# A sparse gate table built with matmuls: one-hots per token on GpSimd and the product into H with tokens innermost

## The chip, the cores and the metric

The kernel runs on one core of a Trainium2 chip. The metric is device time in microseconds (us) of that core, the median of three runs.

## The reference, cut to what matters

The program is one decoder layer of 256 tokens and 1024 channels: a token mixer (attention branches, projections), a layer norm, then a retrieval over 128 x 128 = 16384 single-neuron experts, and a second layer norm. The change lies in the retrieval:

```python
s_top, i_top = lax.top_k(s, K)                      # K = 16 of 128 keys, twice (p = 0, 1), 8 heads
cand = s_top[:, :, 0, :, None] + s_top[:, :, 1, None, :]
best, pos = lax.top_k(cand, K)                      # 16 experts (i, j) per token and head
gate = jax.nn.softmax(best, axis=-1)
hid = gelu(x . u_tab[expert])                       # one number per token and expert
out = sum over the experts of gate * hid * v_tab[expert]
```

The kernel doesn't gather. It computes `hid` for all 16384 experts (dense), builds for each token n the 128 x 128 table G[j, i], the sum of the gates of the token's 128 picks (8 heads x 16) that chose expert (i, j), multiplies `hid` by it, and multiplies the product by all of `v_tab`.

## The kernel before, in words

Five engines run their own instruction streams, ordered by semaphores only. The stages that matter here are three.

- Stage U (128 tiles of `u_tab`). SP loads a tile into `raw`, ScalarE rounds it into `whi` (`split_hi`, L471), VectorE and GpSimd subtract to get `wlo` (`split_lo`, L728 on VectorE for 768 columns, L323 on GpSimd for 256), and TensorE does three matmuls per product (L1173 to L1175). ScalarE writes gelu into `H[j, i, n]`, laid out per partition j as 128 rows i of 256 tokens n, so that neighbouring i lie 1024 bytes apart and neighbouring n 4 bytes. VectorE does the top-k between.
- The gate stage. At its start VectorE copies the transposed picks from PSUM to `selT` (i and j of every pick, one pick per partition, tokens in the free dimension, bf16) and `gateT` (L1104, L1105). Then it goes by blocks of 8 tokens (`BLK`), 32 in all. For a block, VectorE's `hots` (L1066) compares a bf16 iota, stored eight times over (`iota8`), with i and j of the picks, one instruction of 2048 elements that writes both one-hots into `raw_ij` with the token innermost. GpSimd's `scale_j` (L435) multiplies the j one-hots of six tokens by the gate and writes them as fp32 in token order into `hot_j`; ScalarE's `scale_hots` does this for the other two tokens (L673, after copying their gates, L669) and casts the i one-hots into `hot_i` (L670). TensorE's `gate_tables` (L1444) does one 128x128x128 fp32 matmul per token, `hot_j` stationary and `hot_i` moving, into two PSUM banks of a block (the trace shows two records per matmul, so 16 per block). VectorE's `into_h` (L1079) multiplies the 8 x 128 numbers of the block into `H`, walking i innermost in PSUM and in `H`.
- Stage V (128 tiles of `v_tab`): ScalarE and VectorE split `H` into `hhi` and `hlo`, TensorE does L1464 to L1466.

`hot_i` and `hot_j` have two buffers each (`HOTS`), the PSUM side four (`GB`), `raw_ij` two. The hot buffers lie on the memory of `ahi` and `alo`, the stationary side of stage U, so they are written only after the last tile of U (`tiles_used` of `T_V`). A buffer is free again when the block's matmuls are done (`g_done`). In VectorE's loop `hots(n+3)` stands before `into_h(n+1)`. Beside the first blocks run the splits of the first three tiles of V. Stage V begins when the last block's matmuls are issued, `g_used` says that block 28's product is in `H`, and `first_hi` and `first_lo` (the split of the first 128 tokens, L702 and L1119) are there.

Of the kernel before, what the change touches and what calls it, by code (L numbers as in the profile page):

```python
# [23 lines left out]
BF16 = mybir.dt.bfloat16  # L24
U32 = mybir.dt.uint32
ACT = mybir.ActivationFunctionType
AX = mybir.AxisListType

P = 128
SEQ, D = 256, 1024  # L30
# [4 lines left out]
AHEAD = NS - 1  # L35
# [7 lines left out]
PH, NK, TOPK = 8, 128, 16  # L43
# [109 lines left out]
def layer(nc, x, xT, w_lr, w_tiles_in, w_tiles_out, w_tiles_q, w_tiles_u, w_tiles_v, w_decay,  # L153
# [5 lines left out]
    def place(name, shape, dt=F32, alias=None):  # L159
# [3 lines left out]
        if alias is None:  # L163
# [64 lines left out]
    selT = place("selT", [P, 2, SEQ], BF16)  # L228
    gateT = place("gateT", [P, SEQ])
    iota8 = place("iota8", [P, P, BLK], BF16)  # L230
    gate8 = place("gate8", [P, HOTS, BLK])
    gdiff = place("gdiff", [P, NT * P])
    gsum = place("gsum", [P, NT * PH])
    hot_at = at[0]
# [14 lines left out]
    raw_ij = [place(f"raw_ij{b}", [P, 2, P, BLK], BF16, alias=hot_at + b * hot_size) for b in range(HOTS)]  # L249
    at[0] = max(at[0], hot_at + 2 * hot_size)  # L250
# [21 lines left out]
             "sc_copied hid_used r_neg r_exp half_done sel_done sel_tp selT_done iota8_ready hot_ready "  # L272
             "j_scaled hots_wide g_done g_used first_hi first_lo w_hi w_lo out_ready stored dve_own "
# [9 lines left out]
    def spare_hold(e, sem, value):  # L283
        hold(e, sem, value, S["spare"])
# [32 lines left out]
    def _(pool):  # L317
# [98 lines left out]
        pool.wait_ge(S["ln_done"], 2)  # L416
        pool.tensor_copy(iota8[:, :, :], iota[:, :, None].to_broadcast([P, P, BLK])).then_inc(S["iota8_ready"], 1)
# [6 lines left out]
        def scale_j(n, b, i=None):  # L424

            if i is None:
                pool.wait_ge(S["hot_ready"], n + 1)
                if n >= HOTS:
                    pool.wait_ge(S["g_done"], n + 1 - HOTS)
                g = gateT[:, n * BLK:n * BLK + POOL_TOKS]  # L430
            else:
                pool.wait_ge(S["hot_ready"], i * GB + (b + 1))
                spare_hold(pool, S["g_done"], i * GB + (b + 1 - HOTS))
                g = gateT[:, bass.ds(i * (GB * BLK) + b * BLK, POOL_TOKS)]
            pool.tensor_tensor(hot_j[b % HOTS][:, 0:POOL_TOKS, :],  # L435
                               raw_ij[b % HOTS][:, 1, :, 0:POOL_TOKS].rearrange("p j n -> p n j"),
                               g[:, :, None].to_broadcast([P, POOL_TOKS, P]), ALU.mult)\
                .then_inc(S["j_scaled"], 1)
# [3 lines left out]
        for n in range(GB):  # L442
            scale_j(n, n)
            if n == 1:
                split_lo(Tile(T_V + AHEAD - 1))
        with pool.Fori(1, SEQ // BLK // GB) as i:
            for b in range(GB):
                scale_j(None, b, i)
# [16 lines left out]
    def _(act):  # L465
# [192 lines left out]
        def scale_hots(n, b, i=None):  # L658

            if i is None:  # L660
                act.wait_ge(S["hot_ready"], n + 1)
                if n >= HOTS:
                    act.wait_ge(S["g_done"], n + 1 - HOTS)
                g = gateT[:, n * BLK + POOL_TOKS:(n + 1) * BLK]
            else:
                act.wait_ge(S["hot_ready"], i * GB + (b + 1))
                spare_hold(act, S["g_done"], i * GB + (b + 1 - HOTS))
                g = gateT[:, bass.ds(i * (GB * BLK) + (b * BLK + POOL_TOKS), BLK - POOL_TOKS)]
            act.activation(gate8[:, b % HOTS, 0:BLK - POOL_TOKS], g, ACT.Copy).then_inc(S["act_own"], 1)  # L669
            act.activation(hot_i[b % HOTS][:, :, :], raw_ij[b % HOTS][:, 0, :, :].rearrange("p i n -> p n i"), ACT.Copy)  # L670
            act.wait_ge(S["act_own"], own.n + n + 1 if i is None else i * GB + (own.n + b + 1))
            for k in range(POOL_TOKS, BLK):
                last = act.activation(hot_j[b % HOTS][:, k, :], raw_ij[b % HOTS][:, 1, :, k], ACT.Copy,  # L673
                                      scale=gate8[:, b % HOTS, k - POOL_TOKS:k - POOL_TOKS + 1])
            last.then_inc(S["hots_wide"], 1)

        act.wait_ge(S["selT_done"], 1)
        act.wait_ge(S["tiles_used"], T_V)
        for n in range(GB):
            scale_hots(n, n)  # L680
            if n == 1:
                split_hi(Tile(T_V + AHEAD - 1))
        with act.Fori(1, SEQ // BLK // GB) as i:
            for b in range(GB):
                scale_hots(None, b, i)
# [29 lines left out]
        own.n += SEQ // BLK  # L715
# [6 lines left out]
    def _(dve):  # L722
# [333 lines left out]
        def hots(n, b, i=None):  # L1056

            if i is not None:

                spare_hold(dve, S["hots_wide"], i * GB + (b + 1 - HOTS))  # L1060
                spare_hold(dve, S["j_scaled"], i * GB + (b + 1 - HOTS))
            elif n >= HOTS:
                dve.wait_ge(S["hots_wide"], n + 1 - HOTS)
                dve.wait_ge(S["j_scaled"], n + 1 - HOTS)
            toks = slice(n * BLK, (n + 1) * BLK) if i is None else bass.ds(i * (GB * BLK) + b * BLK, BLK)
            dve.tensor_tensor(raw_ij[b % HOTS][:, :, :, :], iota8[:, None, :, :].to_broadcast([P, 2, P, BLK]),  # L1066
                              selT[:, :, toks][:, :, None, :].to_broadcast([P, 2, P, BLK]), ALU.is_equal)\
                .then_inc(S["hot_ready"], 1)

        def into_h(n, b, i=None):  # L1070

            if i is None:
                dve.wait_ge(S["g_done"], n + 1)
            else:
                spare_hold(dve, S["g_done"], i * GB + (b + 1))
            toks = slice(n * BLK, (n + 1) * BLK) if i is None else bass.ds(i * (GB * BLK) + b * BLK, BLK)
            hv = H[:, :, toks].rearrange("p i n -> p n i")
            g = ps[:, 2 * (b % GB):2 * (b % GB) + 2, :].rearrange("p b (n i) -> p (b n) i", i=NK)
            dve.tensor_tensor(hv, hv, g, ALU.mult).then_inc(S["g_used"], 1)  # L1079
# [27 lines left out]
        dve.wait_ge(S["iota8_ready"], 1)  # L1107
        hots(0, 0)
        hots(1, 1)
        split_lo(Tile(T_V))  # L1110
        hots(2, 2)
# [11 lines left out]
        into_h(0, 0)  # L1123
        with dve.Fori(0, SEQ // BLK // GB - 1) as i:
            for b in range(GB):
                hots(b + LAG, b + LAG, i)
                into_h(b + 1, b + 1, i)
        hots(SEQ // BLK - 1, GB - 1)
        into_h(SEQ // BLK - 3, 1)
        into_h(SEQ // BLK - 2, 2)  # L1130
        dve.wait_ge(S["j_scaled"], SEQ // BLK)
        dve.wait_ge(S["hots_wide"], SEQ // BLK)
        first_lo(0)
        into_h(SEQ // BLK - 1, 3)
# [30 lines left out]
    def _(pe):  # L1165
# [268 lines left out]
        def gate_tables(n, b, i=None):  # L1434

            if i is None:
                pe.wait_ge(S["hots_wide"], n + 1)
                pe.wait_ge(S["j_scaled"], n + 1)
            else:
                pe.wait_ge(S["hots_wide"], i * GB + (b + 1))  # L1440
                pe.wait_ge(S["j_scaled"], i * GB + (b + 1))
                pe.wait_ge(S["g_used"], i * GB + (b + 1 - GB))
# [112 lines left out]
```

## Time and profile before

| | |
|---|---|
| Time, median of 3 runs | 1191.5 us (1191.3 to 1192.95) |
| Span of the profiled execution | 1190.3 us |
| Own time of the profiled execution | not listed apart from its span |
| TensorE busy | 1099.9 us (92%) |
| VectorE busy | 824.0 us (69%) |
| ScalarE busy | 623.0 us (52%) |
| GpSimd busy | 549.6 us (46%) |
| Mean granted TensorE clock | 0.989 |
| Gate stage, last matmul of U to first of V | 700.1 to 817.5 us |

The span runs from the first instruction to the last and is 1.2 us below the median of the runs, which also hold what lies around it. Engines are PE (TensorE), DVE (VectorE), ACT (ScalarE), POOL (GpSimd) and SP. A row of a group gives line, engine, operation, output and inputs, shapes, count, then busy us and mean ns of one, then the idle time in front of the instructions and who ended it. A row of a timeline gives the start and the length of an instruction or of a merged run of them (x2, x16).

### The profile page before, as it was taken

How to read it: one execution, taken by the hardware profiler on the slowest of the kernel's cores; microseconds unless marked ns; L12 is line 12 of the kernel's file. 1: busy time of each engine (PE TensorE's matmuls, PEld its weight loads, DVE VectorE, ACT ScalarE, POOL GpSimd, SP SyncE). 2: the span in 40 equal slices, each digit the busy share in tenths (PEclk: the TensorE clock that was granted, in tenths of full speed). 3: DMA queues.
4: the chain of work that ended last, by engine and by line, in shares of the span. 5: the costliest groups of instructions: out<-in, count | busy, mean ns of one | idle time of the engine just before them, and what ended most of it. 6: DMA issues, size and time to landing. Idle time of an engine off the chain costs nothing.

```text
span 1190.3 us, 21974 instructions
## 1 busy us (share of the span) xinstructions
PE 1099.9 (92%) x6734; PEld 971.3 (82%) x6734; DVE 824.0 (69%) x1329; ACT 623.0 (52%) x882; POOL 549.6 (46%) x419
## 2 busy tenths in 40 slices
PE   6999999978999999999999975557999999999995
PEld 5888887658999999999999965556888888888884
DVE  4348654564467777787777899997666666666666
ACT  4357544543455555545555578886445454454452
POOL 5474345453434333333333345554555555555554
PEclk9999999998999999999999999999999999999998
DMA  6654443343455555555555520003555555555552
GB/s 208 228 195 142 142 162 122 124 142 106 159 173 180 179 190 178 179 189 178 181 185 179 181 102 1 0 0 106 178 193 182 188 193 179 192 190 181 193 185 97
DMA packets 52456, 186.34 MB, mean 157 GB/s; under 512 B 6208, under 2 KB 6592, under 8 KB 52432
## 3 DMA queue, kind: packets, MB, share of 16 engines
q1 hardware_dynamic: 51584, 182.87, 46.1%
q0 software_dynamic: 848, 3.15, 0.7%
q8 instruction: 15, 0.25, 0.1%
q14 instruction: 9, 0.07, 0.0%
HBM read 184.94 MB, written 1.05 MB: 156 GB/s over the span
## 4 chain that ended last, share of the span: by engine, by line
PE 80%; DVE 7%; issue 6%; ACT 3%; DMA 2%; POOL 2%; DVEq 0%; ACTq 0%; SPq 0%; POOLq 0%
PE ps L1173 15%; PE ps L1175 15%; PE ps L1174 15%; PE ps L1464 10%; PE ps L1466 10%; PE ps L1465 10%; PE ps L1444 2%; DVE raw_ij L1066 2%; DMA raw<-w_tiles_in 1%; ACT hot_j L673 1%; PE ps L1213 1%; POOL wlo L323 1%; ACT whi L471 1%; DVE H L1079 1%; DVE wlo L728 1%
## 5 line engine op out<-in xcount | busy, mean ns | idle before, releaser
L323 POOL TENSOR_TENSOR wlo<-raw,whi 128x256 fp32r<-128x256 f32 x341 | 445.2, 1306 | 567.2 <-ACT whi L471 566.1
L471 ACT ACTIVATE whi<-raw 128x1024 fp32r<-128x1024 f32 x344 | 365.0, 1061 | 474.3 <-DMA raw<-w_tiles_v 178.3
L728 DVE TENSOR_TENSOR wlo<-raw,whi 128x768 fp32r<-128x768 f32 x341 | 339.1, 995 | 281.0 <-ACT whi L471 264.2
L1173 PE MATMUL ps<-ahi,whi 128*128 128x256 f32 x1152 | 328.3, 285 | 2.7 <-DVE alo L975 1.4
L1175 PE MATMUL ps<-ahi,wlo 128*128 128x256 f32 x1152 | 326.7, 284 | 0.0
L1174 PE MATMUL ps<-alo,whi 128*128 128x256 f32 x1152 | 326.7, 284 | 0.0
L1173 PEld LDWEIGHTS ps<-ahi,whi 128*128 128x128 f32 x1152 | 221.9, 193 | 3.3 <-DVE alo L975 1.8
L1174 PEld LDWEIGHTS ps<-alo,whi 128*128 128x128 f32 x1152 | 221.9, 193 | 0.0
L1175 PEld LDWEIGHTS ps<-ahi,wlo 128*128 128x128 f32 x1152 | 221.8, 192 | 0.0
L1464 PE MATMUL ps<-whi,hhi 128*128 128x512 f32 x512 | 202.5, 395 | 2.5 <-POOL wlo L323 2.5
L1465 PE MATMUL ps<-wlo,hhi 128*128 128x512 f32 x512 | 202.2, 395 | 0.0
L1466 PE MATMUL ps<-whi,hlo 128*128 128x512 f32 x512 | 202.2, 395 | 0.0
L1173 PE MATMUL ps<-whi,ahi 128*128 128x512 f32 x288 | 117.1, 407 | 11.4 <-POOL wlo L323 10.2
L1146 DVE TENSOR_TENSOR hlo<-H,hhi 128x256 fp32r<-128x256 f32 x125 | 118.2, 946 | 0.5 <-ACT hhi L696 0.5
L1464 PEld LDWEIGHTS ps<-whi,hhi 128*128 128x128 f32 x512 | 96.0, 187 | 26.5 <-DVE wlo L728 2.2
L1466 PEld LDWEIGHTS ps<-whi,hlo 128*128 128x128 f32 x512 | 96.0, 187 | 23.6
L1465 PEld LDWEIGHTS ps<-wlo,hhi 128*128 128x128 f32 x512 | 96.0, 187 | 23.4
L1444 PE MATMUL ps<-hot_i,hot_j 128*128 128x128 f32 x512 | 66.8, 285 | 50.8 <-ACT hot_j L673 49.1
L1175 PE MATMUL ps<-whi,alo 128*128 128x512 f32 x288 | 113.4, 394 | 0.0
L1174 PE MATMUL ps<-wlo,ahi 128*128 128x512 f32 x288 | 113.2, 393 | 0.0
L1444 PEld LDWEIGHTS ps<-hot_i,hot_j 128*128 128x128 f32 x512 | 61.1, 196 | 56.5 <-issue 25.6
L435 POOL TENSOR_TENSOR hot_j<-raw_ij,gateT 128x768 f32<-128x768 bf16 x32 | 62.9, 1968 | 49.2 <-DVE raw_ij L1066 47.6
(193 smaller groups left out, 1032.8 us busy)
## 6 DMA issues: line engine op xcount, KB each, us to landing
raw<-w_tiles_u SPq DMA_DIRECT2D x128, 512.0 KB, 3.3
raw<-w_tiles_v SPq DMA_DIRECT2D x128, 512.0 KB, 3.3
raw<-w_tiles_in SPq DMA_DIRECT2D x64, 512.0 KB, 3.3
raw<-w_tiles_q SPq DMA_DIRECT2D x16, 512.0 KB, 3.3
raw<-w_tiles_out SPq DMA_DIRECT2D x8, 512.0 KB, 3.3
xraw<-xT SPq DMA_DIRECT2D x4, 256.0 KB, 6.2
xt<-x POOLq DMA_DIRECT2D x1, 1024.0 KB, 5.7
out<-xt SPq DMA_DIRECT2D x4, 256.0 KB, 2.1
```

Source lines behind the costliest of these rows:

```text
L323: pool.tensor_tensor(wlo[:, tile.slot, DVE_COLS:], raw[:, tile.slot, DVE_COLS:], whi[:, tile.slot, DVE_COLS:].bitcast(F32), ALU.subtract)\
L435: pool.tensor_tensor(hot_j[b % HOTS][:, 0:POOL_TOKS, :], raw_ij[b % HOTS][:, 1, :, 0:POOL_TOKS].rearrange("p j n -> p n j"), g[:, :, None] ...
L471: act.activation(whi[:, tile.slot, :], raw[:, tile.slot, :], ACT.Copy)\
L728: dve.tensor_tensor(wlo[:, tile.slot, 0:DVE_COLS], raw[:, tile.slot, 0:DVE_COLS], whi[:, tile.slot, 0:DVE_COLS].bitcast(F32), ALU.subtract)\
L1146: dve.tensor_tensor(hlo[:, tile.slot, :], src, hhi[:, tile.slot, :].bitcast(F32), ALU.subtract)\
L1173: pe.matmul(out, ah, bh, start=start, stop=False)
L1174: pe.matmul(out, ah, bl, start=False, stop=False)
L1175: return pe.matmul(out, al, bh, start=False, stop=stop)
L1444: last = pe.matmul(ps[:, 2 * b + k // 4, (k % 4) * P:(k % 4 + 1) * P], hot_j[b % HOTS][:, k, :], hot_i[b % HOTS][:, k, :], start=True, sto ...
L1464: pe.matmul(o, hh, wh, start=start, stop=False)
L1465: pe.matmul(o, hh, wl, start=False, stop=False)
L1466: last = pe.matmul(o, hl, wh, start=False, stop=stop)
```

## The change

The one-hots get another form and other makers. GpSimd makes each token's `hot_i` in one instruction of 128 elements: compare the fp32 iota with the token's i, a per-partition scalar, and multiply by its gate, another per-partition scalar. That is eight instructions per block, 256 in all. VectorE makes `hot_j` of a block with one fp32 compare of 1024 elements, straight into the matmul's buffer and no longer with the gate. ScalarE has no part in the stage. `selT` is fp32; `iota8`, `gate8` and `raw_ij` go. VectorE's first compares now wait for the last tile of U too, and the splits of V's first tiles stand behind them. `into_h` walks the tokens innermost: in `H` runs of 8 neighbouring fp32 (32 bytes), in PSUM steps of 128 fp32 (512 bytes). It stands ahead of `hots(n+2)`. Both loops are unrolled. TensorE's matmuls are the same.

```diff
@@ -225,13 +225,10 @@
-    selT = place("selT", [P, 2, SEQ], BF16)
+    selT = place("selT", [P, 2, SEQ])
-    iota8 = place("iota8", [P, P, BLK], BF16)
-    gate8 = place("gate8", [P, HOTS, BLK])
-    hot_at = at[0]
...
@@ -413,39 +408,28 @@
         for m in range(T_Q, T_Q + 4):
             split_lo(Tile(m + AHEAD))
-        pool.wait_ge(S["ln_done"], 2)
-        pool.tensor_copy(iota8[:, :, :], iota[:, :, None].to_broadcast([P, P, BLK])).then_inc(S["iota8_ready"], 1)
         with pool.Fori(1, (T_V - T_Q) // NS - 1) as i:
             for k in range(NS):
                 split_lo(Tile(T_Q + k, i, NS).plus(AHEAD))
         for m in range(T_V - NS, T_V - 1):
             split_lo(Tile(m + AHEAD))
-        def scale_j(n, b, i=None):
-
-            if i is None:
-                pool.wait_ge(S["hot_ready"], n + 1)
-                if n >= HOTS:
-                    pool.wait_ge(S["g_done"], n + 1 - HOTS)
-                g = gateT[:, n * BLK:n * BLK + POOL_TOKS]
-            else:
-                pool.wait_ge(S["hot_ready"], i * GB + (b + 1))
-                spare_hold(pool, S["g_done"], i * GB + (b + 1 - HOTS))
-                g = gateT[:, bass.ds(i * (GB * BLK) + b * BLK, POOL_TOKS)]
-            pool.tensor_tensor(hot_j[b % HOTS][:, 0:POOL_TOKS, :],
-                               raw_ij[b % HOTS][:, 1, :, 0:POOL_TOKS].rearrange("p j n -> p n j"),
-                               g[:, :, None].to_broadcast([P, POOL_TOKS, P]), ALU.mult)\
-                .then_inc(S["j_scaled"], 1)
+        def gated_hots(n):
+
+            if n >= HOTS:
+                pool.wait_ge(S["g_done"], n + 1 - HOTS)
+            for k in range(BLK):
+                tok = n * BLK + k
+                last = pool.tensor_scalar(hot_i[n % HOTS][:, k, :], iota[:, :], selT[:, 0, tok:tok + 1],
+                                          gateT[:, tok:tok + 1], ALU.is_equal, ALU.mult)
+            last.then_inc(S["hot_i_ready"], 1)
         pool.wait_ge(S["selT_done"], 1)
         pool.wait_ge(S["tiles_used"], T_V)
-        for n in range(GB):
-            scale_j(n, n)
+        for n in range(SEQ // BLK):
+            gated_hots(n)
             if n == 1:
                 split_lo(Tile(T_V + AHEAD - 1))
-        with pool.Fori(1, SEQ // BLK // GB) as i:
-            for b in range(GB):
-                scale_j(None, b, i)
         pool.wait_ge(S["g_used"], SEQ // BLK)
         pool.dma_start(g2b[:, :], ln2_g.to_broadcast([P, D])).then_inc(S["in_ln2"], 16)
...
@@ -655,34 +639,7 @@
                 act.wait_ge(S["r_neg"], 1)
                 act.activation(gdiff[:, :], gdiff[:, :], ACT.Exp).then_inc(S["r_exp"], 1)
-        def scale_hots(n, b, i=None):
-
-            if i is None:
-                act.wait_ge(S["hot_ready"], n + 1)
-                if n >= HOTS:
-                    act.wait_ge(S["g_done"], n + 1 - HOTS)
-                g = gateT[:, n * BLK + POOL_TOKS:(n + 1) * BLK]
-            else:
-                act.wait_ge(S["hot_ready"], i * GB + (b + 1))
-                spare_hold(act, S["g_done"], i * GB + (b + 1 - HOTS))
-                g = gateT[:, bass.ds(i * (GB * BLK) + (b * BLK + POOL_TOKS), BLK - POOL_TOKS)]
-            act.activation(gate8[:, b % HOTS, 0:BLK - POOL_TOKS], g, ACT.Copy).then_inc(S["act_own"], 1)
-            act.activation(hot_i[b % HOTS][:, :, :], raw_ij[b % HOTS][:, 0, :, :].rearrange("p i n -> p n i"), ACT.Copy)
-            act.wait_ge(S["act_own"], own.n + n + 1 if i is None else i * GB + (own.n + b + 1))
-            for k in range(POOL_TOKS, BLK):
-                last = act.activation(hot_j[b % HOTS][:, k, :], raw_ij[b % HOTS][:, 1, :, k], ACT.Copy,
-                                      scale=gate8[:, b % HOTS, k - POOL_TOKS:k - POOL_TOKS + 1])
-            last.then_inc(S["hots_wide"], 1)
-
-        act.wait_ge(S["selT_done"], 1)
-        act.wait_ge(S["tiles_used"], T_V)
-        for n in range(GB):
-            scale_hots(n, n)
-            if n == 1:
-                split_hi(Tile(T_V + AHEAD - 1))
-        with act.Fori(1, SEQ // BLK // GB) as i:
-            for b in range(GB):
-                scale_hots(None, b, i)
+        split_hi(Tile(T_V + AHEAD - 1))
         def split_h(tile):
...
@@ -1053,29 +1009,20 @@
         vals = by_head(sel[:, 2, :])
-        def hots(n, b, i=None):
-            if i is not None:
-                spare_hold(dve, S["hots_wide"], i * GB + (b + 1 - HOTS))
-                spare_hold(dve, S["j_scaled"], i * GB + (b + 1 - HOTS))
-            elif n >= HOTS:
-                dve.wait_ge(S["hots_wide"], n + 1 - HOTS)
-                dve.wait_ge(S["j_scaled"], n + 1 - HOTS)
-            toks = slice(n * BLK, (n + 1) * BLK) if i is None else bass.ds(i * (GB * BLK) + b * BLK, BLK)
-            dve.tensor_tensor(raw_ij[b % HOTS][:, :, :, :], iota8[:, None, :, :].to_broadcast([P, 2, P, BLK]),
-                              selT[:, :, toks][:, :, None, :].to_broadcast([P, 2, P, BLK]), ALU.is_equal)\
-                .then_inc(S["hot_ready"], 1)
-        def into_h(n, b, i=None):
-            if i is None:
-                dve.wait_ge(S["g_done"], n + 1)
-            else:
-                spare_hold(dve, S["g_done"], i * GB + (b + 1))
-            toks = slice(n * BLK, (n + 1) * BLK) if i is None else bass.ds(i * (GB * BLK) + b * BLK, BLK)
-            hv = H[:, :, toks].rearrange("p i n -> p n i")
-            g = ps[:, 2 * (b % GB):2 * (b % GB) + 2, :].rearrange("p b (n i) -> p (b n) i", i=NK)
+        def hots(n):
+            if n >= HOTS:
+                dve.wait_ge(S["g_done"], n + 1 - HOTS)
+            dve.tensor_tensor(hot_j[n % HOTS][:, :, :], iota[:, None, :].to_broadcast([P, BLK, P]),
+                              selT[:, 1, n * BLK:(n + 1) * BLK][:, :, None].to_broadcast([P, BLK, P]), ALU.is_equal)\
+                .then_inc(S["hot_j_ready"], 1)
+        def into_h(n):
+            dve.wait_ge(S["g_done"], n + 1)
+            b = n % GB
+            hv = H[:, :, n * BLK:(n + 1) * BLK]
+            g = ps[:, 2 * b:2 * b + 2, :].rearrange("p b (n i) -> p i (b n)", i=NK)
             dve.tensor_tensor(hv, hv, g, ALU.mult).then_inc(S["g_used"], 1)
@@ -1104,11 +1051,10 @@
-        dve.wait_ge(S["iota8_ready"], 1)
-        hots(0, 0)
-        hots(1, 1)
+        dve.wait_ge(S["tiles_used"], T_V)
+        hots(0)
+        hots(1)
-        hots(2, 2)
@@ -1120,18 +1066,12 @@
-        into_h(0, 0)
-        with dve.Fori(0, SEQ // BLK // GB - 1) as i:
-            for b in range(GB):
-                hots(b + LAG, b + LAG, i)
-                into_h(b + 1, b + 1, i)
-        hots(SEQ // BLK - 1, GB - 1)
-        into_h(SEQ // BLK - 3, 1)
-        into_h(SEQ // BLK - 2, 2)
-        dve.wait_ge(S["j_scaled"], SEQ // BLK)
-        dve.wait_ge(S["hots_wide"], SEQ // BLK)
-        first_lo(0)
-        into_h(SEQ // BLK - 1, 3)
+        for n in range(SEQ // BLK):
+            if n == SEQ // BLK - 1:
+                first_lo(0)
+            into_h(n)
+            if n + HOTS < SEQ // BLK:
+                hots(n + HOTS)
@@ -1434,11 +1374,11 @@
-                pe.wait_ge(S["hots_wide"], n + 1)
-                pe.wait_ge(S["j_scaled"], n + 1)
+                pe.wait_ge(S["hot_i_ready"], n + 1)
+                pe.wait_ge(S["hot_j_ready"], n + 1)
-                pe.wait_ge(S["hots_wide"], i * GB + (b + 1))
-                pe.wait_ge(S["j_scaled"], i * GB + (b + 1))
+                pe.wait_ge(S["hot_i_ready"], i * GB + (b + 1))
+                pe.wait_ge(S["hot_j_ready"], i * GB + (b + 1))

```

## Rows read from the trace of the kernel before

**Rows 1.** Page: span; VectorE's busy tenths in 40 slices of 29.8 us.

```profile
span 1190.3 us, 21974 instructions
DVE  4348654564467777787777899997666666666666
```

**Rows 2.** Groups by line and shape, 700.1 to 817.8 us, the gate stage.

```profile
L1079 DVE TENSOR_TENSOR H<-H,ps 128x1024 f32 x28 | 71.6, 2558 | 0.0
L670 ACT ACTIVATE hot_i<-raw_ij 128x1024 f32<-128x1024 bf16 x32 | 69.5, 2172 | 0.0
L1444 PE MATMUL ps<-hot_i,hot_j 128*128 128x128 f32 x512 | 66.8, 285 | 50.8 <-ACT hot_j L673 49.1 <-POOL hot_j L435 1.7
L435 POOL TENSOR_TENSOR hot_j<-raw_ij,gateT 128x768 f32<-128x768 bf16 x32 | 62.9, 1968 | 49.2 <-DVE raw_ij L1066 47.6 <-PE ps L1175 1.6
L1066 DVE TENSOR_TENSOR raw_ij<-iota,selT 128x2048 bf16<-128x2048 bf16 x31 | 39.7, 1281 | 0.1
```

**Rows 3.** Timeline of VectorE, one block of eight tokens.

```profile
717.80 1.20 DVE L1066 TENSOR_TENSOR raw_ij<-iota,selT 128x2048 bf16<-128x2048 bf16 x1
718.94 2.53 DVE L1079 TENSOR_TENSOR H<-H,ps 128x1024 f32 x1
721.39 1.20 DVE L1066 TENSOR_TENSOR raw_ij<-iota,selT 128x2048 bf16<-128x2048 bf16 x1
```

**Rows 4.** Waits, 718.9 to 815.7 us: total us, times, longest.

```profile
PE ps L1444 <- ACT hot_j L673: 41.9, 27, 1.9
POOL hot_j L435 <- DVE raw_ij L1066: 44.5, 27, 1.7
```

**Rows 5.** Timeline of TensorE, start and end of the gate stage.

```profile
703.78 5.44 PE L1444 MATMUL ps<-hot_i,hot_j 128*128 128x128 f32 x32 [3.65 <-ACT hot_j L673]
710.88 2.02 PE L1444 MATMUL ps<-hot_i,hot_j 128*128 128x128 f32 x16 [1.66 <-POOL hot_j L435]
...
815.72 2.05 PE L1444 MATMUL ps<-hot_i,hot_j 128*128 128x128 f32 x16 [1.48 <-ACT hot_j L673]
817.53 0.48 PE L1464 MATMUL ps<-whi,hhi 128*128 128x512 f32 x1
```

**Rows 6.** Timelines of VectorE and GpSimd where both are at work.

```profile
11.83 0.73 POOL L323 TENSOR_TENSOR wlo<-raw,whi 128x256 fp32r<-128x256 f32 x1 [0.42 <-ACT whi L471]
11.88 1.50 DVE L728 TENSOR_TENSOR wlo<-raw,whi 128x768 fp32r<-128x768 f32 x1
...
285.81 0.96 DVE L728 TENSOR_TENSOR wlo<-raw,whi 128x768 fp32r<-128x768 f32 x1 [0.20 <-ACT whi L471]
285.86 1.51 POOL L323 TENSOR_TENSOR wlo<-raw,whi 128x256 fp32r<-128x256 f32 x1 [1.60 <-ACT whi L471]
...
703.46 2.71 DVE L1066 TENSOR_TENSOR raw_ij<-iota,selT 128x2048 bf16<-128x2048 bf16 x1
...
719.30 1.93 POOL L435 TENSOR_TENSOR hot_j<-raw_ij,gateT 128x768 f32<-128x768 bf16 x1 [1.59 <-DVE raw_ij L1066]
```

**Rows 7.** GpSimd: short instructions (timeline), then a long one (groups).

```profile
13.26 0.20 POOL L333 MEMSET chunk_mask<- 128x128 f32 x1
15.12 0.54 POOL L342 TENSOR_SCALAR_AFFINE_SELECT causal<-causal 128x128 f32<-128x128 f32 x2
15.61 0.29 POOL L344 TENSOR_SCALAR_AFFINE_SELECT chunk_mask<-chunk_mask 128x128 f32<-128x128 f32 x1
...
L407 POOL TENSOR_TENSOR wlo<-raw,whi 128x1024 fp32r<-128x1024 f32 x3 | 7.0, 2362 | 1.1 <-ACT whi L471 1.1
```

**Rows 8.** VectorE, 1024 elements in plain order (groups by line).

```profile
L785 DVE TENSOR_TENSOR gla<-gla 128x1024 f32<-128x1024 f32 x1 | 1.2, 1221 | 0.0
L869 DVE COPY state<-ps 128x1024 f32<-128x1024 f32 x1 | 1.2, 1218 | 0.0
```

**Rows 9.** Stretches: us, busy us of PE, PEld, DVE, ACT, POOL, PEclk, DMA, GB/s.

```profile
704.00:711.00 7.00, 5.34 (x33) 5.17 (x33) 6.73 (x5) 6.40 (x8) 4.47 (x3) 0.76 0.00 0
712.00:816.00 104.00, 58.52 (x459) 53.10 (x458) 104.00 (x58) 90.65 (x119) 56.13 (x29) 1.00 0.00 0
```

More of the change, by code:

```diff
@@ L247, in layer @@
     hot16 = place("hot16", [P, 2, TOPK, TOPK])
-    raw_ij = [place(f"raw_ij{b}", [P, 2, P, BLK], BF16, alias=hot_at + b * hot_size) for b in range(HOTS)]
-    at[0] = max(at[0], hot_at + 2 * hot_size)
     assert at[0] <= nc.sbuf_usable_end, at[0]
@@ L271, in layer @@
              "ln_shift ln_scaled ln_times_g ln_sqrt ln_done x1_tp ln_done0 out_ready0 q_copied sc_done "
-             "sc_copied hid_used r_neg r_exp half_done sel_done sel_tp selT_done iota8_ready hot_ready "
-             "j_scaled hots_wide g_done g_used first_hi first_lo w_hi w_lo out_ready stored dve_own "
+             "sc_copied hid_used r_neg r_exp half_done sel_done sel_tp selT_done hot_i_ready hot_j_ready "
+             "g_done g_used first_hi first_lo w_hi w_lo out_ready stored dve_own "
              "pool_own act_own spare ").split()
@@ L714, in _ @@
             split_hi(Tile(m))
-        own.n += SEQ // BLK
         own.do(act.activation(gate_warm[:, :], ident[:, 0:1], ACT.Sqrt))
```

## The prediction

> **What bounds the kernel now.** I read the page first: a span of 1190.3 us in which VectorE, 0.4 to 0.8 busy elsewhere, stands at 9 in slices 24 to 27 of 40, from 685 to 804 us [rows 1]. That is the gate stage, so I grouped its instructions by line. The largest group is the product into H: 2558 ns for 1024 elements, where plain work of that size takes 1218 to 1221 ns [rows 2, 8]. The two other engines that feed the matmuls are shorter per block: ScalarE 2172 ns for the i one-hots, GpSimd 1968 ns [rows 2].
>
> The timeline of VectorE then gives the beat. A compare starts at 717.80, the product at 718.94, the next compare at 721.39: 1.14 + 2.45 = 3.59 us per block, and nothing between them [rows 3]. From 712 to 816 us it is busy for 104.00 of 104 us, TensorE for 58.5 [rows 9]. The waits have to be read with care: TensorE waits 41.9 us for ScalarE's last j one-hot, 27 times, but GpSimd waits 44.5 us for VectorE's compare, also 27 times [rows 4]. ScalarE is late because the compare is late. So the stage is bound by VectorE, and ends with it: block 0's matmuls start at 703.78, block 2's at 710.88, the last block's at 815.72, and stage V follows at 817.53 without a gap [rows 5]. Stages U and V keep TensorE full and the change doesn't touch them. What the last block's start moves by, the kernel moves by. Call this start T; now T = 815.72.
>
> **Product into H.** The same 1024 elements; in H the step of 1024 bytes becomes runs of 32 bytes, in PSUM runs of 512 bytes become single elements 512 bytes apart. Nothing in the trace reads PSUM so. Lower end: 1.14 us on the beat, by the plain rows (1218 ns less the overlap of about 0.07 us that [rows 3] show) [rows 8]. Upper end: as slow as the strided H now, 2.45 us. I take the lower one: the outlying step was on two accesses (read and write of H) and would be on one.
>
> The Trainium skill (Advanced Engine Details and Errata, Memory Cachelines) speaks against it: SBUF wants two hits per 16-byte line, which the new H order gives, but PSUM's lines hold only two fp32, and each element now falls in another line. That page gives no price for VectorE. By the upper end, which stands for it, VectorE's beat would stay near 3.6 us; this is rival C below.
>
> **The compare.** VectorE's bf16 compare made 2048 results in 1.14 us [rows 3]; the fp32 one makes 1024 in 1221 ns, 1.15 us on the beat [rows 8]. Nothing gained there. With the product at 1.14, VectorE alone needs 2.3 us per block and would no longer be the bound.
>
> **ScalarE and TensorE.** ScalarE's 2172 ns and its gate copies and scaled copies leave; they stood beside VectorE, so they are worth nothing by themselves. TensorE needs 2.05 us per block, as before [rows 5]. The removed `iota8` copy lies in another stage, beside GpSimd's waits: nothing. Copies of `selT` to fp32 instead of bf16: nothing.
>
> **GpSimd.** This is the new step that counts: 256 instructions of 128 elements. Call the beat of one t. Nearest row in kind: the affine select, one 128x128 input, a compare and a choice. Two of them and the start of the next lie 0.49 us apart, so t = 0.245; a memset of the shape is busy 0.20 [rows 7]. That is the lower end (0.2 to 0.245), since a tensor_scalar also fetches two per-partition scalars and does two operations. Upper end: a two-input instruction. 256 elements take 0.73 us [rows 6], 1024 take 2.36 [rows 7], so 2.1 ns per element over 0.19 us fixed, 0.46 us for 128. I take 0.35, the middle between the nearest row in kind and this one.
>
> By the Trainium skill (GPSIMD Engine Reference, Performance pitfalls for Q7 kernels) each small read command costs about 102 cycles that aren't pipelined, an estimate of 85 ns at 1.2 GHz; were each pointer scalar one, t would be 0.245 + 0.17 = 0.415 and the sum below +27 us. No row here shows a pointer scalar on GpSimd.
>
> **The two together.** Where VectorE reads two SBUF tensors and GpSimd reads SBUF, one stands still for the other. GpSimd began at 11.83 and took 0.73; VectorE's 768-column subtraction began at 11.88 and took 1.50 instead of 0.96. At 285.81 VectorE was first: it took 0.96, and GpSimd's subtraction 1.51, so 0.78 lost [rows 6]. The compare does this too: at 703.46 it took 2.71 us for 1.20, behind a GpSimd instruction [rows 6]. The product into H, with one operand in PSUM, doesn't: GpSimd's 1.93 us at 719.30 lay wholly beside it [rows 3, 6]. Now GpSimd scales only after the compare, so they hardly meet. After the change GpSimd works without a pause and each block's compare takes its access away for 0.78 + 256 x 1.04 ns = 1.04 us (256 elements more than the subtraction). So GpSimd's beat is 8t + 1.04, against VectorE's 2.3 plus at most one t. GpSimd becomes the bound.
>
> **The sum.** GpSimd starts at 700.2, when U's last matmul has let go of the buffers (before too). Its first two blocks share the access with two compares and three V-tile subtractions of VectorE: 2 x 1.04 + 3 x 0.78 = 4.4 us, and behind block 1 stands its own subtraction, 0.74. Then 30 blocks: T = 700.2 + 4.4 + 0.74 + 16t + 30 x (8t + 1.04) = 736.5 + 256t. At t = 0.35: 30 blocks of 3.84 us, T = 826.1, that is +10.4 us. The point of no change is t = 0.309. TensorE's start of block 0 falls from 703.78 to about 708; the granted clock, which read 0.76 over the first matmuls after the pause and 1.00 behind them [rows 9], may read low there again, but block 0's matmuls aren't what GpSimd waits for. Behind T nothing is late: ScalarE is free, so `first_hi` and `first_lo` stand ready, and `g_used` for block 28 is long given. Span 1190.3 + 10.4 = 1200.7; with the 1.2 us between this span and the median, 1201.9. I forecast 1202 us.
>
> **Rivals.**
> - A, the forecast: t between 0.32 and 0.39, 1194 to 1213 us. For: the rows of kind and of size stand on either side.
> - B, a costly small instruction, t from 0.40 to 0.46 or above: T = 839 to 854, 1215 to 1230 us. For: every GpSimd row has 0.1 to 0.2 us fixed, and two scalars add to it. Against: the affine selects.
> - C, PSUM's steps as slow as H's were, and t small enough for VectorE to be the bound: 1.15 + 2.45, plus on average half a GpSimd instruction of waiting, 3.6 to 3.8 us per block. Its first product starts near 710 instead of 708.2; 30 blocks later 818 to 824, 1194 to 1200 us. For: the strided H shows that VectorE pays for steps.
> - D, the other side: t = 0.245 or less, as the affine select, and PSUM's steps free. GpSimd's beat is 3.0 us, T = 799.2, 1175 us; at t = 0.29, 1186.6. It decides below t = 0.309. For: the nearest row in kind. Against: it has no scalars to fetch.
> - E, the two engines don't hold each other, since GpSimd's reads are short: 8t = 2.8 us at t = 0.35 without the 4.4 and the 30 x 1.04, 1166 us. Against: [rows 6] in both directions.
>
> **Chances.** A 0.34, B 0.20, C 0.16, D 0.24, E 0.06. A change of 0.2% (2.4 us) is about what can be told from none. Slower by more: A 0.31, B 0.20, C 0.12, together 0.63; within: 0.03 of A, 0.03 of C, 0.01 of D, 0.07; faster: D 0.23, E 0.06 and 0.01 of C, 0.30. The range goes from D's 1175 to the upper end of B, 1230, leaving out E, the quickest of D and what lies above t = 0.46; A's own range stands above.
>
> **What would show it.** The group of GpSimd's tensor_scalar with 256 entries: its beat t from the timeline where VectorE is in its product (0.35; below 0.309 with short products: D). The group of the product: 1.2 us or near 2.5 (C). The compare: 1.2 us alone, up to 1.6 behind a GpSimd instruction, and one GpSimd instruction in eight about 1 us longer than the others (none longer: E). VectorE's busy time over the stage's middle, 2.3 to 2.6 of 3.8 us, and TensorE waiting for GpSimd at every block. T near 826. It would be wrong if stage V began with a gap, or if the matmuls themselves took longer.

## The result and the profile after

The changed kernel takes 1302.4 us (median of 4 runs, 1300.9 to 1302.9) against 1192.0 us of the kernel before: ratio 1.092, 95% interval 1.0905 to 1.0936. It is 110 us slower. The forecast was 1202 us, with a range from 1175 to 1230; the direction was right, the size wrong by a factor of about ten (110 us for 10). The profiled execution took 1302.85 us, its span is 1300.9.

The page of the changed kernel, its span, VectorE's busy tenths and the granted TensorE clock in 40 slices (32.5 us each):

```profile
span 1300.9 us, 21638 instructions
DVE  3448553654677777787786333333366666666666
PEclk9999999979999999999998655677899999999998
```

VectorE, at 9 in four slices of 29.8 us before [rows 1], is at 3 in seven slices of 32.5. The granted clock of the stage falls to 0.5 to 0.7 of full speed, where it was 1.00 [rows 9]; from 760 to 800 us it is 0.50, the lower of its two levels, where TensorE stands idle for about 3.1 us before each block's matmuls. Groups by line and shape over the gate stage (695 to 950 us), which answer to [rows 2]:

```profile
L423 POOL TENSOR_SCALAR hot_i<-iota,selT,gateT 128x128 f32<-128x128 f32 x256 | 224.6, 898 | 1.7 <-PE ps L1115 1.7
L1384 PE MATMUL ps<-hot_i,hot_j 128*128 128x128 f32 x512 | 117.0, 421 | 111.9 <-POOL hot_i L423 111.9
L1026 DVE TENSOR_TENSOR H<-H,ps 128x1024 f32<-128x1024 f32 x32 | 39.1, 1221 | 151.2 <-PE ps L1384 151.2
L1016 DVE TENSOR_TENSOR hot_j<-iota,selT 128x1024 f32<-128x1024 f32 x32 | 39.0, 1221 | 1.8 <-PE ps L1115 1.8
```

GpSimd's 256 short instructions are busy for 224.6 us; TensorE waits for them 111.9 us in all, 32 times, once for each block. The product into H is down from 2558 to 1221 ns, and the fp32 compare takes 1221 ns. The chain of work that ended last, from 720 to 880 us, is one piece, GpSimd from end to end:

```profile
719.80 160.86 POOL hot_i L423 x185
```

The timeline of TensorE answers to [rows 5]; the two rows of GpSimd under it show blocks 0 and 1 and the start of the steady part:

```profile
711.44 3.75 PE L1384 MATMUL ps<-hot_i,hot_j 128*128 128x128 f32 x16 [10.59 <-POOL hot_i L423]
718.38 3.48 PE L1384 MATMUL ps<-hot_i,hot_j 128*128 128x128 f32 x16 [3.19 <-POOL hot_i L423]
...
926.40 3.30 PE L1384 MATMUL ps<-hot_i,hot_j 128*128 128x128 f32 x16 [2.58 <-POOL hot_i L423]
929.35 0.77 PE L1404 MATMUL ps<-whi,hhi 128*128 128x512 f32 x1
```

```profile
701.06 17.27 POOL L423 TENSOR_SCALAR hot_i<-iota,selT,gateT 128x128 f32<-128x128 f32 x16 [1.68 <-PE ps L1115]
719.01 7.30 POOL L423 TENSOR_SCALAR hot_i<-iota,selT,gateT 128x128 f32<-128x128 f32 x8
```

T, the start of the last block's matmuls, went from 815.72 to 926.40 us, by 110.7 us: the difference of the spans (110.6). Behind T the passage to stage V is 1.1 us longer and stage V itself 1.2 us shorter, which cancel. From 719.01 on, 30 blocks took 207.4 us, 6.91 each, where they took 3.59. GpSimd's single instructions around one compare of VectorE, from its timeline:

```profile
766.39 1.49 POOL L423 TENSOR_SCALAR hot_i<-iota,selT,gateT 128x128 f32<-128x128 f32 x1
767.87 0.79 POOL L423 TENSOR_SCALAR hot_i<-iota,selT,gateT 128x128 f32<-128x128 f32 x1
768.65 0.79 POOL L423 TENSOR_SCALAR hot_i<-iota,selT,gateT 128x128 f32<-128x128 f32 x1
```

and VectorE's in the same block:

```profile
766.00 1.22 DVE L1016 TENSOR_TENSOR hot_j<-iota,selT 128x1024 f32<-128x1024 f32 x1
771.84 1.22 DVE L1026 TENSOR_TENSOR H<-H,ps 128x1024 f32<-128x1024 f32 x1 [4.62 <-PE ps L1384]
```

The beat t, from start to start, is 0.773 us (767.87 to 768.65 and on), not 0.35. The instruction that meets the compare is 0.70 longer: it ends at 767.88, 0.66 us after the compare. Eight beats and one such delay are 6.9 us. VectorE's compare doesn't wait here.

The first instruction of all was held longest. VectorE's two compares and its first subtraction for stage V stand one behind the other:

```profile
701.06 3.58 POOL L423 TENSOR_SCALAR hot_i<-iota,selT,gateT 128x128 f32<-128x128 f32 x1 [1.68 <-PE ps L1115]
700.89 2.36 DVE L1016 TENSOR_TENSOR hot_j<-iota,selT 128x1024 f32<-128x1024 f32 x2 [1.84 <-PE ps L1115]
703.17 0.95 DVE L684 TENSOR_TENSOR wlo<-raw,whi 128x768 fp32r<-128x768 f32 x1
```

GpSimd's 3.58 us end at 704.64, 0.52 us after the subtraction.

### The profile page after: what moved, and what is told of

Its sections match the earlier page's. It is cut to its first block, busy times and chain, and to the rows that moved or that the text cites. A ratio compares the mean times of both kernels' runs of the same rounds, so it can differ in the third digit from the quotient of the medians.

```text
span 1300.9 us, 21638 instructions
## 1 busy us (share of the span) xinstructions
PE 1151.7 (89%) x6734; PEld 1020.0 (78%) x6734; DVE 781.2 (60%) x1329; ACT 522.9 (40%) x754; POOL 707.2 (54%) x642
## 4 chain that ended last, share of the span: by engine, by line
PE 73%; POOL 18%; DVE 4%; DMA 2%; issue 1%; ACT 1%; DVEq 0%; SPq 0%; POOLq 0%
POOL hot_i L423 17%; PE ps L1113 14%; PE ps L1115 14%; PE ps L1114 14%; PE ps L1404 9%; PE ps L1406 9%; PE ps L1405 9%; PE ps L1153 1%; DMA raw<-w_tiles_in 1%; POOL wlo L318 1%; DVE wlo L684 1%; ACT whi L455 1%; PE ps L1340 1%; DVE xt L900 1%; PE ps L1229 0%
## 5 line engine op out<-in xcount | busy, mean ns | idle before, releaser
L423 POOL TENSOR_SCALAR hot_i<-iota,selT,gateT 128x128 f32<-128x128 f32 x256 | 224.6, 898 | 1.7 <-PE ps L1115 1.7
L1384 PE MATMUL ps<-hot_i,hot_j 128*128 128x128 f32 x512 | 117.0, 421 | 111.9 <-POOL hot_i L423 111.9
L1384 PEld LDWEIGHTS ps<-hot_i,hot_j 128*128 128x128 f32 x512 | 108.7, 323 | 120.0 <-issue 84.6
L1026 DVE TENSOR_TENSOR H<-H,ps 128x1024 f32<-128x1024 f32 x32 | 39.1, 1221 | 151.2 <-PE ps L1384 151.2
```

Source lines behind the costliest of these rows:

```text
L423: last = pool.tensor_scalar(hot_i[n % HOTS][:, k, :], iota[:, :], selT[:, 0, tok:tok + 1], gateT[:, tok:tok + 1], ALU.is_equal, ALU.mult)
L1384: last = pe.matmul(ps[:, 2 * b + k // 4, (k % 4) * P:(k % 4 + 1) * P], hot_j[b % HOTS][:, k, :], hot_i[b % HOTS][:, k, :], start=True, sto ...
```

## The experiments

Theory after the result: GpSimd's instruction costs 0.77 us by itself, and this is what the forecast missed. Rivals: the exclusion between VectorE and GpSimd, the fallen TensorE clock, the new walk through PSUM, or the sheer number of instructions. Where no ratio is given the time is that of one run, to be set beside the 1192.0 to 1192.5 us that the kernel before took on the same chips.

**e1_forms: what 128 elements cost on GpSimd, by form.** GpSimd's loop in the changed kernel takes another form of instruction from block to block, eight forms in turn (code shortened):

```diff
+ f == 0: tensor_scalar(o, iota, si, g, is_equal, mult)      f == 4: tensor_scalar(o, iota, si, g, mult, add)
+ f == 1: tensor_scalar(o, iota, si, None, is_equal)         f == 5: tensor_tensor(o, iota, ident, mult)
+ f == 2: tensor_scalar(o, iota, 3.0, 0.5, is_equal, mult)   f == 6: tensor_copy(o, iota)
+ f == 3: tensor_scalar(o, iota, 3.0, None, is_equal)        f == 7: as 0, four tokens' width (512) at once
```

> The changed kernel, with GpSimd's instruction in eight forms, one form per block in turn (four blocks each): both per-token scalars; one per-token scalar and one operation; two constants and two operations; one constant and one operation; both scalars with multiply and add; a product of two 128-element tensors; a plain copy; and both scalars with four tokens' worth of elements (512) in one instruction. The gates are right in the first form only, so its output leaves the others' gates out. If fetching the two per-token scalars is what makes 128 elements cost 0.77 us, the forms with constants and the copy fall to 0.25 to 0.35 us, the one with one scalar lies halfway (0.5), and the 512-element form takes about 1.1 us. If the two operations cost 5 ns per element, the 512-element form takes 3.1 us and constants don't help. If a compare is slow by itself, the multiply-and-add form is short, and both compares with constants stay near 0.77. Whole kernel: by the first, some 60 us less than 1302; by the second, within 30 us of it, since the copy and the product alone get shorter.

1238.7 us. The forms by their lines (ns: least, median, longest; where the longest is far above the median, the instruction met VectorE's compare, and the one of 3582 met what VectorE does at the start of the stage; L426 is form 0, then in order up to L440, form 7):

```profile
L426 POOL TENSOR_SCALAR hot_i<-iota,selT,gateT x32: 785/788/3582, 700.3 to 829.2; 128x128 f32<-128x128 f32 x32
L428 POOL TENSOR_SCALAR hot_i<-iota,selT x32: 592/601/607, 710.4 to 834.0; 128x128 f32<-128x128 f32 x32
L430 POOL TENSOR_SCALAR hot_i<-iota x32: 634/638/1711, 715.7 to 840.9; 128x128 f32<-128x128 f32 x32
L432 POOL TENSOR_SCALAR hot_i<-iota x32: 521/524/529, 722.4 to 844.9; 128x128 f32<-128x128 f32 x32
L434 POOL TENSOR_SCALAR hot_i<-iota,selT,gateT x32: 437/445/1527, 726.4 to 849.5; 128x128 f32<-128x128 f32 x32
L436 POOL TENSOR_TENSOR hot_i<-iota,ident x32: 447/452/1477, 731.9 to 854.8; 128x128 f32<-128x128 f32 x32
L438 POOL COPY hot_i<-iota x32: 285/289/1305, 735.9 to 856.8; 128x128 f32<-128x128 f32 x32
L440 POOL TENSOR_SCALAR hot_i<-iota,selT,gateT x4: 2077/2081/2087, 738.9 to 859.3; 128x512 f32<-128x512 f32 x4
```

A per-token scalar costs 0.075 us each (638 to 788 for two, 524 to 601 for one): the smaller part. The 512-element form takes 2.08 us, so an element costs (2081 - 788) / 384 = 3.4 ns, and 128 of them 0.43 us; 0.36 us is fixed. Each of the three theories holds only in part: the scalars cost something, the elements cost 3.4 instead of 5 ns, and multiply-and-add with the same two scalars is short (0.445), though the compares with constants take 0.52 and 0.64, not 0.77. The whole time, 64 us less than the changed kernel, fell by luck where the first theory had put it (60 less), whose durations failed.

**e5_forms2: is it the compare?** The same loop with other forms (code shortened).

```diff
+ f == 0: (mult, mult)   f == 1: (is_equal, add)   f == 2: (add, mult)   f == 3: (subtract, mult)     two per-token scalars
+ f == 6: (add) alone with a constant              f == 7: (mult, add) with constants
+ f == 4: (mult, add), two scalars, 512 wide       f == 5: (is_equal) alone, one scalar, 512 wide
```

> More forms of GpSimd's instruction, one per block in turn; all gates are wrong, so the output leaves the gating out. Known so far for 128 elements: compare and multiply with two per-token scalars 0.79 us, compare alone with one 0.60, multiply alone with one 0.60, multiply and add with two 0.45. If the compare has a slow path and multiply-then-add a special short one, then multiply-multiply, add-multiply and subtract-multiply cost 0.75 to 0.8 like the compare; if only compares are slow, they cost 0.45. The 512-element forms give the slope: multiply-and-add 1.0 us or less (0.45 + 384 x 1.1 to 1.5 ns), the lone compare about 1.6 us (0.60 + 384 x 2.5 ns).

1240.0 us. Forms 0, 1, 2, 3, 6, 7, 4, 5 in this order:

```profile
L428 POOL TENSOR_SCALAR hot_i<-iota,selT,gateT x32: 446/449/3216, 700.6 to 830.8; 128x128 f32<-128x128 f32 x32
L430 POOL TENSOR_SCALAR hot_i<-iota,selT,gateT x32: 784/792/1706, 708.3 to 836.7; 128x128 f32<-128x128 f32 x32
L432 POOL TENSOR_SCALAR hot_i<-iota,selT,gateT x32: 447/452/458, 716.1 to 841.2; 128x128 f32<-128x128 f32 x32
L434 POOL TENSOR_SCALAR hot_i<-iota,selT,gateT x32: 790/794/1867, 719.6 to 848.9; 128x128 f32<-128x128 f32 x32
L436 POOL TENSOR_SCALAR hot_i<-iota x32: 523/526/1286, 735.5 to 862.3; 128x128 f32<-128x128 f32 x32
L438 POOL TENSOR_SCALAR hot_i<-iota x32: 296/298/298, 741.0 to 864.7; 128x128 f32<-128x128 f32 x32
L442 POOL TENSOR_SCALAR hot_i<-iota,selT,gateT x8: 770/772/774, 727.9 to 850.5; 128x512 f32<-128x512 f32 x8
L444 POOL TENSOR_SCALAR hot_i<-iota,selT x8: 1571/1870/2170, 731.8 to 855.2; 128x512 f32<-128x512 f32 x8
```

Both readings I had written down are wrong in part. Two operations that are both adds or multiplies run at 0.45 us, and multiply-and-add at (772 - 445) / 384 = 0.85 ns per element; a subtract or a compare in the first place gives 0.79 us (the 3.4 ns per element of e1 were measured for compare-and-multiply alone). The lone compare costs (1571 - 601) / 384 = 2.5 ns per element, as expected. A lone add with a constant (0.526) costs as much as a lone compare (0.524), and more than multiply-and-add with constants (0.298). So it isn't the compare as such: of the `tensor_scalar` forms tried, pairs of add and multiply are quick, all others slow. Why is not shown.

**f1_mult_add: does the sum hold when only this duration changes?**

```diff
-  gateT[:, tok:tok + 1], ALU.is_equal, ALU.mult)
+  gateT[:, tok:tok + 1], ALU.mult, ALU.add)
```

> The changed kernel with multiply-and-add in place of compare-and-multiply in GpSimd's 256 instructions, all else the same (the gated one-hots are left out, the numbers are wrong). The instruction lasts 0.45 us instead of 0.79. If this duration alone was mis-sized in the forecast's sum and its structure holds, the block is 8 x 0.43 + 0.71 = 4.15 us, the last block's matmuls start near 839 and the kernel takes 1212 to 1219 us. If something else holds the block near 6.9 us (the granted TensorE clock, VectorE), it stays above 1250.

1222.6 us, 80 us less than the changed kernel, by the two operations of GpSimd's instruction alone (0.453 us median). The last block's matmuls start at 847.60. It misses the expected window by 4 us: the blocks take some 4.5 us, not 4.15. The trace says why. An instruction of GpSimd that meets a compare lasts 1.41 us here, so it loses 0.96 and not 0.71:

```profile
749.63 1.31 DVE L1016 TENSOR_TENSOR hot_j<-iota,selT 128x1024 f32<-128x1024 f32 x1
749.85 1.41 POOL L423 TENSOR_SCALAR hot_i<-iota,selT,gateT 128x128 f32<-128x128 f32 x1
```

With its 1.04 us per block the forecast's own sum fits here: at this run's beat of 0.431 us it gives T = 736.5 + 110.3 = 846.8, measured 847.60. The rivals (clock, VectorE) are out as the cause of the 6.9: nothing else holds the block there. This kernel is still 31 us slower than the one before: 0.43 lies above the forecast's point of no change, 0.309, and so does every form with two per-token scalars that was tried.

**e2_no_compare: what VectorE's compare takes from GpSimd.**

```diff
             if n >= HOTS:
-                dve.wait_ge(S["g_done"], n + 1 - HOTS)
+                return
```

> The changed kernel without VectorE's compares after the first two blocks (the j one-hots of 30 blocks are left out; all else runs). If VectorE's compare, which reads two SBUF tensors, holds GpSimd back by the 0.71 us that one instruction in eight is longer (1.49 instead of 0.79), the block falls from 6.9 to 6.2 us and the kernel by 30 x 0.71 = 21 us, to 1281. If the longer instruction has another cause (the wait at the block's start), it stays, and the time stays at 1302.

(TensorE's wait for the missing compares is taken out as well.) 1281.7 us, 20.7 less (21 expected). GpSimd's instructions follow one another without a long one:

```profile
759.89 20.98 POOL L423 TENSOR_SCALAR hot_i<-iota,selT,gateT 128x128 f32<-128x128 f32 x27
```

The exclusion costs 0.7 us per block, a tenth of the block's 6.9 us.

**e3_old_walk: the product into H walked as before.**

```diff
-            hv = H[:, :, n * BLK:(n + 1) * BLK]
-            g = ps[:, 2 * b:2 * b + 2, :].rearrange("p b (n i) -> p i (b n)", i=NK)
+            hv = H[:, :, n * BLK:(n + 1) * BLK].rearrange("p i n -> p n i")
+            g = ps[:, 2 * b:2 * b + 2, :].rearrange("p b (n i) -> p (b n) i", i=NK)
```

> The changed kernel with the product into H walked as before (i innermost: H in steps of 1024 bytes, PSUM contiguous). If the new walk's gain lies off the path, hidden behind GpSimd, the product goes from 1.22 back to about 2.5 us and the kernel stays within 3 us of 1302, since VectorE idles 4.5 us in every block. If the walk is part of the loss or of a gain on the path, the kernel moves by 30 x 1.3 = 39 us.

1306.8 us. The product takes 2392 ns again, and of the 38 us that this adds to VectorE only 4.5 reach the end. That is more than the 3 us I had expected, and it is one run. The blocks there come by turns 6.2 and 8.1 us apart (TensorE's starts at 910.11, 916.29, 924.40), so the compare meets GpSimd at another place:

```profile
759.59 1.21 DVE L1016 TENSOR_TENSOR hot_j<-iota,selT 128x1024 f32<-128x1024 f32 x1
759.52 1.85 POOL L423 TENSOR_SCALAR hot_i<-iota,selT,gateT 128x128 f32<-128x128 f32 x1
L423 POOL TENSOR_SCALAR hot_i<-iota,selT,gateT 128x128 f32<-128x128 f32 x256 | 229.8, 911 | 1.7 <-PE ps L1115 1.7
```

Where a compare starts together with a GpSimd instruction, that instruction loses 1.06 us instead of 0.70. All 256 are busy for 229.8 us instead of 224.6, 5.2 more, and the first began 1.1 us earlier (699.9, not 701.06): together the 4.1 us by which the last block's matmuls start later (930.51). So the walk reaches the end through the exclusion, not through VectorE's own time.

**b1_new_walk: this part alone, in the kernel before.** The same two lines in the other direction, in the kernel before.

> The kernel before with this one part of the change alone: the product into H with tokens innermost. If VectorE is what bounds the block before (1.14 + 2.45 = 3.59 us), its work falls to 2.3 us and ScalarE becomes the bound with about 3.15 us per block: 30 x 0.2 to 0.45 us less, 1178 to 1186 us. If ScalarE was the bound all along, as the last wait names it, nothing moves: 1191.5.

1181.5 us, ratio 0.9912 (0.9895 to 0.9928): inside the expected window, but not for the reason given (ScalarE as the next bound). VectorE and GpSimd, one block:

```profile
741.66 2.25 DVE L1066 TENSOR_TENSOR raw_ij<-iota,selT 128x2048 bf16<-128x2048 bf16 x1
743.83 1.21 DVE L1079 TENSOR_TENSOR H<-H,ps 128x1024 f32 x1
744.96 2.19 DVE L1066 TENSOR_TENSOR raw_ij<-iota,selT 128x2048 bf16<-128x2048 bf16 x1
```

```profile
744.19 1.88 POOL L435 TENSOR_TENSOR hot_j<-raw_ij,gateT 128x768 f32<-128x768 bf16 x1 [1.37 <-DVE raw_ij L1066]
```

The product fell from 2.5 to 1.21, but the compare rose from 1.20 [rows 3] to 2.2: it now starts while GpSimd is in its 1.88 us, and stands until that is over. Of 1.3 us saved per block, 1.0 went into a new wait.

**b2_new_walk_7: is it this wait, or ScalarE?** b1 with `POOL_TOKS = 7`.

> The kernel before with the new walk of the product (as b1, 1181.5 us) and GpSimd scaling seven tokens instead of six, ScalarE one instead of two. In b1 VectorE's bf16 compare takes 2.2 us instead of 1.20 beside GpSimd's 1.88. If it is this exclusion that sets b1's block of 3.25 us (1.88 + 1.14 + 0.23), seven tokens (2.2 us) make it 3.55 us: about 1190. If ScalarE sets it (0.11 + 2.0 + 0.93 + 0.2), it falls by 0.4 us per block: about 1169.

1189.9 us: the exclusion's number. ScalarE had less to do (0.9 us idle per block) and the block got longer all the same.

**m1_one_multiply and c1_multiplies: GpSimd only multiplies.** VectorE makes both one-hots with two compares, and GpSimd waits for them (code shortened).

```diff
-            for k in range(BLK):
-                ...
+            last = pool.tensor_tensor(hot_i[..], hot_i[..], gateT[..8 tokens..][:, :, None].to_broadcast([P, BLK, P]), ALU.mult)   # m1
+            for k in range(BLK):                                                                                                  # c1
+                last = pool.tensor_scalar(hot_i[..k..], hot_i[..k..], gateT[:, tok:tok + 1], None, ALU.mult)
```

> The changed kernel with VectorE comparing both i and j (two fp32 compares per block) and GpSimd multiplying the eight i one-hots by their gates in one two-input instruction of 1024 elements. If compares of a short shape are what is dear on GpSimd, it now costs 2.4 us per block, and with VectorE's two compares (2.3 us) apart from it by exclusion the block is 4.7 to 4.9 us: 1225 to 1235 us, 70 less than the changed kernel. If GpSimd's share is dear whatever it does (2.1 ns or more per element plus waiting), the block stays above 6 us: 1270 or more.

> As m1, but GpSimd multiplies token by token: eight instructions of 128 elements with one per-token scalar and one operation. By the forms' run: a copy 0.29 us, a per-token scalar 0.08 more, so 0.36 each, 2.9 us per block, plus 0.7 for each of two compares of VectorE: 4.3 us per block, about 1215 us. If the count of 256 instructions is the cost, whatever they do, it stays within 20 us of 1302.

m1 took 1224.6 us, 78 less than the changed kernel and just under the expected 1225 to 1235: GpSimd's one multiply of 1.90 us (2.4 expected) and one more compare on VectorE stand where eight instructions of 0.79 stood. c1 took 1300.6, where I had expected 1215: a lone multiply with one scalar costs 0.598 us, not the 0.36 that I had put together from a copy and a scalar, and GpSimd besides waits for VectorE (148 of 188 us busy). c1 by itself would have spoken for the rival that the number of instructions is what costs; f1, with the same 256 instructions and 80 us less, speaks against it.

**s1_split521 and s2_split422: a version that beats both.** (Code shortened; s1 deals five tokens to ScalarE, two to GpSimd, one to VectorE; s2 four, two and two.) Each engine makes the gated one-hots of some tokens of a block. ScalarE needs two instructions for one: |i - iota|, then Relu(gate - gate x distance), which is the gate at distance 0 and zero elsewhere.

```diff
+            for k in range(ACT_TOKS):
+                last = act.activation(away[:, n % 3, k, :], iota[:, :], ACT.Abs, bias=selT[:, 0, tok:tok + 1], scale=-1.0)
+            ...
+                last = act.activation(hot_i[n % HOTS][:, k, :], away[:, n % 3, k, :], ACT.Relu,
+                                      bias=gateT[:, tok:tok + 1], scale=gneg[:, tok:tok + 1])
```

> The changed kernel with the eight gated one-hots of a block dealt out: five tokens on ScalarE (Abs of the distance of the iota from i, then Relu of gate minus gate times distance, two instructions per token), one on VectorE (the same compare-and-multiply, as one instruction of its own), two on GpSimd. If GpSimd's 0.77 us per token is the whole loss, its two tokens cost 1.55 + 0.71 us and the block is set by VectorE: compare 1.15, product 1.14, one token 0.2, some waiting: 2.5 to 2.8 us per block. Last block's matmuls near 790 instead of 815.7 before: 1160 to 1172 us. If the exclusion between VectorE and GpSimd or ScalarE's waits cost more than that, the block is 3.2 us or more: 1180 or above.

1185.9 us, ratio 0.9947 (0.993 to 0.9963): slower than expected. ScalarE was full: five Relu in 2.02 and five Abs in 1.55 us, each pair overlapping into a block of 3.38 us.

> As s1 (1185.9 us), with four tokens on ScalarE, two on VectorE, two on GpSimd. In s1 ScalarE ran without a pause: Relu every 0.39 us and Abs every 0.29, 3.4 us per block for five tokens. If that is the bound, four tokens cost 2.7 us, VectorE stands at 1.14 + 1.14 + 2 x 0.3 = 2.9 with some waiting, and the block falls to about 3.0 us: 1185.9 - 30 x 0.4 = 1174 us, range 1168 to 1179. If the exclusion between VectorE and GpSimd or the two buffers set it, it stays at 1183 to 1188.

1168.6 us, ratio to the kernel before 0.9801 (0.9788 to 0.9814), 134 us below the changed kernel, at the quick end of the range expected. The block is about 2.8 us, not 3.0: VectorE's two tokens take 0.52 us on its beat, not 0.6. One stretch of its stage, in the columns of [rows 9], and two rows of VectorE:

```profile
710.00:790.00 80.00, 58.90 (x459) 53.73 (x459) 79.97 (x114) 78.81 (x228) 47.97 (x57) 0.99 0.00 1
```

```profile
743.17 1.21 DVE L1064 TENSOR_TENSOR H<-H,ps 128x1024 f32<-128x1024 f32 x1
...
745.95 1.21 DVE L1064 TENSOR_TENSOR H<-H,ps 128x1024 f32<-128x1024 f32 x1
```

VectorE (79.97 of 80) and ScalarE (78.81) are both full, the clock is back at 0.99. The last block's matmuls start at 793.83, 21.9 us earlier than before.

## Why the prediction was wrong

- **What bounded the kernel.** Right: VectorE's 3.59 us per block. b1 took 1.3 us of it away and gained a third of a microsecond per block.
- **The product into H.** Right at the lower end: 1221 ns, so PSUM in steps of 512 bytes costs VectorE nothing. Rival C falls. The Trainium skill (Advanced Engine Details and Errata, Memory Cachelines) is borne out for SBUF, where steps of 1024 bytes took 2392 to 2558 ns and runs of 32 bytes 1221; its short PSUM lines cost VectorE nothing measurable here.
- **The compare.** Right: 1221 ns, 1.14 on the beat.
- **ScalarE and TensorE.** That ScalarE's leaving is worth nothing by itself no run tests; s1 and s2, where it makes part of the one-hots, beat both kernels. TensorE's 2.05 us per block was wrong, and with it one of the prediction's own signs of being wrong came true: the matmuls took 2.95 to 3.78 us, at a granted clock of 0.5 to 0.7. They are still shorter than GpSimd's 6.9, so only the passage to stage V shows it: from T to its first matmul 2.95 us, 1.81 before.
- **GpSimd's instruction. This is the step that failed:** "Upper end: a two-input instruction ... 0.46 us for 128. I take 0.35". It is 0.773. The bounds were made from rows of other operations: the affine select runs at 0.245, the two-input product at 0.45 (the e1 run confirms that end to 0.01), and I took the slope of 2.1 ns per element for the worst that a short instruction does. A compare-and-multiply does 3.4 ns per element, above either. The whole miss of 100 us is here: 256 x (0.773 - 0.35) = 108 us, less the 8 us of the sum below.
- **The estimate by the Trainium skill** (GPSIMD Engine Reference, Performance pitfalls for Q7 kernels), 0.17 us for the reads of two scalars, was close: they cost 0.15 us in e1. The base of 0.245 under it was what failed: added to the 0.638 with constants it would have given 0.81, where 0.788 was measured. That a scalar is such a read no run shows.
- **The two together.** The exclusion exists (e2: 20.7 us), but costs 0.73 us per block here, not 1.04; where the compare comes at another point of GpSimd's instruction, it is 0.96 or 1.06 (f1, e3). Almost only GpSimd pays it here: the compare stays at 1.22 to 1.26. VectorE pays where GpSimd's instruction is long (b1: 2.2).
- **The sum.** With t = 0.773 it gives T = 736.5 + 197.9 = 934.4; measured 926.4. The 8.0 us between them: 30 x (0.73 - 1.04) = -9.3, the first two blocks' exclusion 4.9 (17.27 less 16 beats of 0.773) instead of 4.4, of which the first instruction has 2.8, and the start at 701.06 instead of 700.2. The structure was right; f1 shows it at a second measured t, where the sum is off by 0.8 us.
- **The rivals.** B had the mechanism (a costly small instruction), with its price cut off at 0.46. D's condition on PSUM came true, its t didn't. E is out by e2 and by the one instruction in eight that is longer.

## What to carry to other kernels

A bound for an operation that the trace doesn't show is no bound if it comes from other operations of the same engine: on GpSimd forms of 128 elements run from 0.29 to 0.79 us, and the pair of operations decides. Multiply the doubt by the count before taking a middle value: 256 instructions turn 0.42 us into 108. The point of no change (0.309 us) was the number to hold the guess against: no form with two per-token scalars that was tried lies under it. And where a freed engine shares something with another (VectorE and GpSimd reading SBUF), look at what it will now run into: b1 gave back 1.0 of 1.3 us that way.

## What the hardware did that I had not expected

- GpSimd's tensor_scalar, fp32, 128 elements: with two operations out of add and multiply 0.445 to 0.452 us with two per-partition scalars and 0.298 with constants, for multiply-and-add 0.85 ns per element more; with is_equal or subtract first and two scalars 0.79 us, for compare-and-multiply 3.4 ns per element more; one operation alone (add, multiply or is_equal) 0.52 to 0.60 us, for is_equal 2.5 ns per element more. A lone add or multiply is slower than a pair of them.
- A short GpSimd instruction that meets a VectorE compare of two SBUF inputs (1.22 us) loses 0.70 us (changed kernel), 0.96 (f1) or 1.06 (e3), by where the compare starts. The first one of the changed kernel took 3.58 us behind two compares and a subtraction in a row. In s2, where VectorE's two short `tensor_scalar` stand between its compares, the first one takes 1.84 us:

```profile
700.44 1.84 POOL L425 TENSOR_SCALAR hot_i<-iota,selT,gateT 128x128 f32<-128x128 f32 x1 [1.68 <-PE ps L1153]
```

- VectorE reads PSUM fp32 in steps of 512 bytes at full rate (1221 ns for 1024 elements), while SBUF in steps of 1024 bytes, read and written, costs 2392 to 2558 ns.
- ScalarE's Relu with scale and bias per partition takes 0.39 us per 128 elements on the beat, Abs with bias and a constant scale 0.29.
